# Earlier score copy, and latents modulated tile by tile beside the last context values

## The chip, the cores and the metric

The kernel runs on one core of a Trainium2 chip. The metric is the time of one execution on the device in microseconds (us). The engines, by the names of the profile, are PE (TensorE: matmuls), DVE (VectorE), ACT (ScalarE), POOL (GpSimd) and SP (SyncE, which here only issues transfers). Each engine runs its own instructions strictly in the order in which they were written. They meet through semaphores: an instruction waits until a counter has reached a value, and all behind it on that engine waits too.

## The reference, cut to what matters

Two blocks are computed on 256 tokens of width 2048. The first is a mixture of gating, dilated and sparse attention, cross attention and an MLP. Its output `x` goes into the second, and this is where the change lies:

```python
sh_m, sc_m, gt_m, sh_f, sc_f, gt_f = _modulation(c)        # silu(c) @ w_ada + b_ada, six parts
h_lat = x * (1.0 + sc_m) + sh_m                             # 256 latents
h_ctx = ctx * (1.0 + csc_m) + csh_m                         # 256 context tokens
q, k, v, log decays, g, p, bg = split(h @ w_in)             # for both; of the context k, v, decays matter
o_c, s_fwd, s_bwd = gla_two_way(context, zero state)        # chunks of 64, both directions
o_l, _, _ = gla_two_way(latents, s_fwd, s_bwd)
...                                                         # pooling branch, gates, norm, SwiGLU FFN (sh_f, sc_f, gt_f)
```

`o = q_inter @ state + scores @ v` within each head: the state's part is first formed as a small matrix of scores, and that matrix is then multiplied with the values.

## The kernel before, in words

**Weights.** All large products take weights that are streamed from memory in chunks of 1 MB (`RW`, five slots) and processed in halves of 512 KB. ACT rounds a half to a high part (`RH`, line 1194), DVE subtracts to get the low part (`RL`, line 2036), and PE multiplies both with the activations `A`, which are a pair of high and low too. One half is the clock of the whole program. `prepare` makes the parts four halves ahead of PE: the high part of half n+4 waits until PE has used half n-1, since there are five buffers. `gemm` is a product with columns of output on the partitions (lines 513 and 518, eight matmuls each). `gemm_n` is used for the values V, has tokens on the partitions and takes the tiles of `A` as stationary operand, two tiles (a pair) per half (lines 554, 556, 561).

**Order.** `schedule` is executed once for each engine and writes its instructions. `run` steps several generators in turn, and each `yield` ends a step, which as a rule holds one half of weights. What an engine writes in step n stands on it beside what the others write in step n. `beside=` is one more lane, stepped first. On ACT the products come ahead of the side work of a step (`weights_first`), on PE and DVE behind it. `slow(lane, 1.42)` steps a lane in two of three steps or so.

**The stretch in question.** After the context's modulation come `k2`, `low_rank`, and then a run of 45 steps: the products V, V, K, V, V of the context, beside four `ctx_head`s of 11 steps each (decays, sums, the state keys of a head, on ACT and DVE). Then the latents are modulated into `A` (`modulate(1, ...)`): for each of eight pairs of tiles DVE scales and shifts (line 2558, two instructions), ACT rounds to the high part (line 1659), DVE subtracts the low part (line 2548). `MODULATED` spreads this over six steps. `q2` then multiplies `A` with the first query weights; its first eight halves are zipped, block 0 and block 1 in turn, so that it needs pairs 0 and 1 for its halves 0 and 1, pairs 2 and 3 for halves 2 and 3, and so on (`need`). ACT waits before the first rounding until the last V product has used all of `A`.

Blocks alternate between two pairs of PSUM banks. A block waits (`block_begins`) until the block two before it is evacuated. After V products ACT does this (line 1690, two copies of 128x512); after `q2` and `k2` DVE does (line 2095) with a copy by ACT (line 1201) ahead of it.

**Fourth modulation sums.** `ada((4,), ...)` sums `silu(c) * w_ada` for one of the six parts: 32 transfers of 512 KB, each followed by one DVE instruction on 128x1024 (lines 2479, 2482). The number in `pauses` is how many steps lie between two of them. SP issues the transfer for item n+2 after item n is done (two slots), in its one queue, between the weight transfers. The result is needed only in the FFN; the lane is emptied before the latent heads.

**Latent heads.** `lat_head(h)` has two directions d; in each PE makes the scores inside chunks and then (line 1045) the scores of the state, in bank 5. ACT copies these from PSUM to `ST` (line 1828), and in the next step PE multiplies them with the state's values (line 1058). Before, the copy stands in the step after line 1045, behind that step's rounding of weights.

Of the kernel before, what the change touches and what calls it, by code (L numbers as in the profile page):

```python
# [129 lines left out]
class Banks:  # L130
# [11 lines left out]
    def next(self, signals=True):  # L142
        i = self.turn[self.at % len(self.turn)]
        self.at += 1
        return self.take(i, signals)
# [72 lines left out]
def chain(*lanes):  # L218
    for lane in lanes:
        yield from lane  # L220
# [8 lines left out]
def idle(n=0):  # L229
    for _ in range(n):  # L230
        yield
# [247 lines left out]
def tensor_program(nc, m, io):  # L479
# [3 lines left out]
    L = Lanes()  # L483
# [502 lines left out]
    def ctx_head(h):  # L986
        decay(0, h)
        decay(1, h)
        yield from idle(11)

# [190 lines left out]
def scalar_program(nc, m, io):  # L1181
# [470 lines left out]

    def modulate(use, tms):
        a.wait_ge(s["used"], num.last_of_a)
        for step in MODULATED:
            for p, low in step:
                if not low:
                    a.wait_ge(s["dm"], 8 * use + p + 1)
                    a.activation(m.A.high(2 * p, 2), pair2(tms[p % 2]), ACT.Copy).then_inc(s["dh"], 1)
            yield  # L1660

    def modulate_ctx():
        yield from modulate(0, m.x3_bufs[2:4])

# [18 lines left out]
    def v2():  # L1683
        n, dst = num.v, m.V[num.v % 2]
        num.v += 1

        def evac(b, g):
# [59 lines left out]
    def ctx_head(h):  # L1747
# [16 lines left out]
        yield  # L1764
        yield
        a.wait_ge(s["ks"], 2 * h + 2)
# [3 lines left out]
    def modulate_lat():  # L1770
        num.last_of_a = num.half
        yield from modulate(1, m.ON)

# [20 lines left out]
    def lat_head(h):  # L1794
# [5 lines left out]
        for d in range(2):  # L1800
# [21 lines left out]
            banks.next()  # L1822
            yield
            yield
        if num.on is not None:
            a.wait_ge(num.on.full, num.on.filled)
        a.wait_ge(s["qs"], 2 * h + 2)
        a.activation(m.ST, st.ap[:, :], ACT.Copy).then_inc(st.empty, 1)
        yield
# [195 lines left out]
def vector_program(nc, m, io):  # L2025
# [620 lines left out]
    def ctx_head(h):  # L2646
# [30 lines left out]
        yield  # L2677
        yield

# [410 lines left out]
def sync_program(nc, m, io):  # L3090
# [140 lines left out]
    L.v2 = lambda: gemm_n(1)  # L3231
    L.ctx_head = lambda h: idle(11)
    L.modulate_lat = L.alpha_x = lambda: idle(6)
# [35 lines left out]
def schedule(L):  # L3269
# [24 lines left out]
    L.low_rank(0)  # L3294
    beside = L.ada((4,), (2.25,))
    heads = chain(idle(1), L.ctx_head(0), L.ctx_head(1), L.ctx_head(2), L.ctx_head(3))
    run(*L.beside(heads, chain(L.v2(), L.v2(), L.k2(0, 2, 2), L.v2(), L.v2())), beside=beside)
    modulated = L.modulate_lat()
    next(modulated)
    run(*L.beside(modulated, L.q2()), beside=beside)  # L3300
    L.low_rank(1)
# [173 lines left out]
```

## Time and profile before

| | us |
|---|---|
| Three runs: median (lowest to highest) | 3023.03 (3022.83 to 3024.53) |
| Profiled execution: its own time | 3025.02 |
| Profiled execution: span of its instructions | 3023.7 |
| PE busy | 2941.7 (97%) |
| DVE busy | 2170.4 (72%) |
| ACT busy | 1454.5 (48%) |
| Mean granted clock of PE, as a share of full speed | 0.989 |

Busy time of PE counts overlapping matmuls once. Its 82 us of idle time lie in a few tens of waits, and the chain that ended last runs through PE for 91% of the span, so a microsecond that PE waits is a microsecond of the kernel's time, unless a later wait absorbs it. Idle time of the other engines costs nothing by itself. A row of a stretch has its bounds, its length, busy time (and number of instructions) of PE, of PE's weight loads, of DVE, ACT and POOL, then PE's granted clock as a share of full speed, the busy share of the DMA engines, and GB/s. A timeline row has the start, the duration from the first instruction's start to the last one's end, and in brackets the idle time before it with what ended it.

### The profile page before, as it was taken

How to read it: one execution, taken by the hardware profiler on the slowest of the kernel's cores; microseconds unless marked ns; L12 is line 12 of the kernel's file. 1: busy time of each engine (PE TensorE's matmuls, PEld its weight loads, DVE VectorE, ACT ScalarE, POOL GpSimd, SP SyncE). 2: the span in 40 equal slices, each digit the busy share in tenths (PEclk: the TensorE clock that was granted, in tenths of full speed). 3: DMA queues.
4: the chain of work that ended last, by engine and by line, in shares of the span. 5: the costliest groups of instructions: out<-in, count | busy, mean ns of one | idle time of the engine just before them, and what ended most of it. 6: DMA issues, size and time to landing. Idle time of an engine off the chain costs nothing.

```text
span 3023.7 us, 40090 instructions
## 1 busy us (share of the span) xinstructions
PE 2941.7 (97%) x16526; PEld 2545.6 (84%) x16526; DVE 2170.4 (72%) x2677; ACT 1454.5 (48%) x1941; POOL 8.5 (0%) x21
## 2 busy tenths in 40 slices
PE   8999999999999999998999999999999999999998
PEld 7888788888888888887887778888878888888886
DVE  5556767889899886789756656558888775555557
ACT  5445555544444444555444444544545444444444
POOL 0000000000000000000000000000000000000000
PEclk9999999999999999999999999999999999999999
DMA  6545234677677785577655445559646765555553
GB/s 251 194 168 195 98 140 151 233 263 260 257 264 265 288 316 208 183 273 273 257 185 181 167 163 190 192 216 344 226 160 251 280 249 183 193 183 193 185 191 112
DMA packets 107237, 648.61 MB, mean 215 GB/s; under 512 B 11920, under 2 KB 11920, under 8 KB 43440
## 3 DMA queue, kind: packets, MB, share of 16 engines
q1 hardware_dynamic: 99936, 621.86, 56.7%
q10 hardware_dynamic: 5184, 16.78, 1.4%
q0 software_dynamic: 1936, 7.41, 0.6%
q8 instruction: 131, 2.15, 0.3%
q14 instruction: 50, 0.41, 0.0%
HBM read 635.52 MB, written 10.49 MB: 214 GB/s over the span
## 4 chain that ended last, share of the span: by engine, by line
PE 91%; DVE 5%; ACT 2%; issue 1%; DMA 1%; SPq 0%; DVEq 0%; ACTq 0%
PE PS L513 50%; PE PS L518 26%; PE PS L554 3%; PE PS L556 3%; PE PS L561 3%; DVE RL L2036 1%; PE PS L791 1%; ACT RH L1194 1%; PE PS L1058 1%; PE PS L930 0%; PE PS L1045 0%; DMA RW<-in_w_ckv 0%; PE PS L976 0%; PE PS L582 0%; PE PS L693 0%
## 5 line engine op out<-in xcount | busy, mean ns | idle before, releaser
L2036 DVE TENSOR_TENSOR RL<-RW,RH 128x1024 fp32r<-128x1024 f32 x974 | 1177.9, 1222 | 544.7 <-ACT RH L1194 538.7
L1194 ACT ACTIVATE RH<-RW 128x1024 fp32r<-128x1024 f32 x974 | 1015.5, 1055 | 768.6 <-PE PS L518 652.0
L513 PE MATMUL PS<-A,RH 128*128 128x512 f32 x4544 | 1162.8, 398 | 35.0 <-ACT RH L1194 10.3
L513 PEld LDWEIGHTS PS<-A,RH 128*128 128x128 f32 x4544 | 827.1, 191 | 193.9 <-issue 37.8
L518 PEld LDWEIGHTS PS<-A,RL 128*128 128x128 f32 x4544 | 624.9, 192 | 45.4
L518 PE MATMUL PS<-A,RL 128*128 128x256 f32 x4544 | 637.9, 284 | 0.0
L513 PE MATMUL PS<-H,RH 128*128 128x512 f32 x2304 | 582.1, 395 | 1.2 <-ACT RH L1194 1.2
L513 PEld LDWEIGHTS PS<-H,RH 128*128 128x128 f32 x2304 | 416.2, 189 | 76.7 <-issue 1.4
L518 PEld LDWEIGHTS PS<-H,RL 128*128 128x128 f32 x2304 | 314.5, 190 | 22.7
L518 PE MATMUL PS<-H,RL 128*128 128x256 f32 x2304 | 321.3, 282 | 0.0
L1201 ACT ACTIVATE LT<-PS 128x512 f32<-128x512 f32 x232 | 138.2, 596 | 326.4 <-PE PS L518 326.3
L2482 DVE SCALAR_TENSOR_TENSOR G<-G,SILT 128x1024 f32<-128x1024 f32 x210 | 263.5, 1278 | 11.8 <-DMA G<-in_w_ada 11.7
L554 PE MATMUL PS<-RH,A 128*128 128x512 f32 x416 | 163.0, 392 | 0.0
L556 PE MATMUL PS<-RH,A 128*128 128x512 f32 x416 | 162.1, 390 | 0.0
L2095 DVE TENSOR_TENSOR G<-PS,LT 128x512 f32<-128x512 f32 x116 | 79.7, 687 | 72.8 <-ACT LT L1201 65.8
L561 PE MATMUL PS<-RL,A 128*128 128x512 f32 x416 | 111.2, 389 | 0.0
L554 PEld LDWEIGHTS PS<-RH,A 128*128 128x128 f32 x416 | 78.1, 188 | 17.8 <-issue 2.0
L561 PEld LDWEIGHTS PS<-RL,A 128*128 128x128 f32 x416 | 78.1, 188 | 16.3
L556 PEld LDWEIGHTS PS<-RH,A 128*128 128x128 f32 x416 | 78.1, 188 | 15.8
L1628 ACT ACTIVATE G<-G 128x512 f32<-128x512 f32 x32 | 20.2, 632 | 131.5 <-DVE G L2515 131.5
L1442 ACT ACTIVATE G<-G,SM 128x256 f32<-128x256 f32 (+1 forms) x56 | 24.8, 443 | 51.6 <-DVE SM L2287 51.6
L2404 DVE TENSOR_TENSOR X<-X,LT 128x512 f32<-128x512 f32 x56 | 38.5, 687 | 15.2 <-ACT LT L1201 15.2
(253 smaller groups left out, 1511.6 us busy)
## 6 DMA issues: line engine op xcount, KB each, us to landing
RW<-in_w_fin SPq DMA_DIRECT2D x88, 1024.0 KB, 4.8
G<-in_w_ada SPq DMA_DIRECT2D x160, 512.0 KB, 5.9
RW<-in_w_up SPq DMA_DIRECT2D x64, 1024.0 KB, 4.9
RW<-in_w_down SPq DMA_DIRECT2D x64, 1024.0 KB, 5.2
RW<-in_w_fout SPq DMA_DIRECT2D x44, 1024.0 KB, 4.7
RW<-in_w_v SPq DMA_DIRECT2D x32, 1024.0 KB, 4.9
RW<-in_w_bg SPq DMA_DIRECT2D x32, 1024.0 KB, 4.8
RW<-in_w_k SPq DMA_DIRECT2D x16, 1024.0 KB, 5.0
```

Source lines behind the costliest of these rows:

```text
L513: t.matmul(pair[mm][:, :], wh[:, k, mm * 128:mm * 128 + 128], x2(4 * c + k)[0], start=first and k == 0, stop=False, skip_group_check=True)
L518: done = t.matmul(pair[mm][:, 0:256], wl[:, k, mm * 128:mm * 128 + 128], x2(4 * c + k)[1], start=False, stop=last and k == 3, skip_group_c ...
L554: t.matmul(out[mm], hi(2 * c + k)[:, rows[mm]], wh[:, k, :], start=first and k == 0, stop=False, skip_group_check=True)
L556: t.matmul(out[mm], lo(2 * c + k)[:, rows[mm]], wh[:, k, :], start=False, stop=False, skip_group_check=True)
L561: done = t.matmul(out[mm], hi(2 * c + k)[:, rows[mm]], wl[:, k, :], start=False, stop=last and k == 1, skip_group_check=True)
L791: done = t.matmul(bk.ap[:, i * 128:i * 128 + 128], v, pt[0:n, j * 128:j * 128 + 128], start=x == 0, stop=x == len(ops) - 1)
L1194: a.activation(m.high(x), m.slot(j)[:, x % 2 * HC:x % 2 * HC + HC], ACT.Copy).then_inc(s["hi"], 1)
L1201: a.activation(pair2(m.LT[g % 2]), m.sum_l[g % 2], ACT.Copy).then_inc(s["lt"], 1)
L2036: v.tensor_tensor(m.low(x), m.slot(j)[:, x % 2 * HC:x % 2 * HC + HC], m.high(x).bitcast(F32), ALU.subtract).then_inc(s["lo"], 1)
L2095: v.tensor_tensor(pair2(out), m.sum_h[g % 2], pair2(m.LT[g % 2]), ALU.add).then_inc(m.pair[g % 2], 1)
L2404: stepped(v.tensor_tensor(x, x, m.LT[g % 2], ALU.add))
L2482: v.scalar_tensor_tensor(acc, m.ada_slot[cb][at], silu, acc, ALU.mult, ALU.add).then_inc(s["av"], 1)
```

## The change

Three things are done.

1. In `lat_head` ACT's copy of the score matrix moves up by one step, into the step in which PE makes the last of these scores (d == 1). The wait for `qs` stays with it.
2. `modulate_lat` no longer follows the context's V products but runs beside the last of them. `ctx_head` has 10 steps instead of 11 (an empty one is gone), so the fourth head ends after step 40, and the modulation takes steps 41 to 46; the last V has its halves in steps 36 to 43, and `q2` begins in step 45. Instead of one wait for the whole product, ACT waits for each pair p until the last V product has used its half p (`num.last_v + p + 1`), which is the half that reads pair p.
3. The pauses of the fourth modulation sums are 3.8 steps for the first ten of the 32, then 1.9, instead of 2.25 throughout.

```diff
     def ctx_head(h):
         decay(0, h)
         decay(1, h)
-        yield from idle(11)
+        yield from idle(10)
...
-    def modulate(use, tms):
-        a.wait_ge(s["used"], num.last_of_a)
+    def modulate(use, tms, free):
         for step in MODULATED:
             for p, low in step:
                 if not low:
+                    a.wait_ge(s["used"], free(p))
                     a.wait_ge(s["dm"], 8 * use + p + 1)
                     a.activation(m.A.high(2 * p, 2), pair2(tms[p % 2]), ACT.Copy).then_inc(s["dh"], 1)
             yield
 
     def modulate_ctx():
-        yield from modulate(0, m.x3_bufs[2:4])
+        yield from modulate(0, m.x3_bufs[2:4], lambda p: num.last_of_a)
...
     def v2():
         n, dst = num.v, m.V[num.v % 2]
         num.v += 1
+        num.last_v = num.half
...
         a.wait_ge(s["ks"], 2 * h + 2)
         a.dma_start(io["state"][h][:, 0:1024], m.KS).then_inc(l["spill"], 16)
...
     def modulate_lat():
-        num.last_of_a = num.half
-        yield from modulate(1, m.ON)
+        yield from modulate(1, m.ON, lambda p: num.last_v + p + 1)
...
             banks.next()
             yield
-            yield
-        if num.on is not None:
-            a.wait_ge(num.on.full, num.on.filled)
-        a.wait_ge(s["qs"], 2 * h + 2)
-        a.activation(m.ST, st.ap[:, :], ACT.Copy).then_inc(st.empty, 1)
+            if d == 1:
+                if num.on is not None:
+                    a.wait_ge(num.on.full, num.on.filled)
+                a.wait_ge(s["qs"], 2 * h + 2)
+                a.activation(m.ST, st.ap[:, :], ACT.Copy).then_inc(st.empty, 1)
+            yield
         yield
...
-    beside = L.ada((4,), (2.25,))
-    heads = chain(idle(1), L.ctx_head(0), L.ctx_head(1), L.ctx_head(2), L.ctx_head(3))
-    run(*L.beside(heads, chain(L.v2(), L.v2(), L.k2(0, 2, 2), L.v2(), L.v2())), beside=beside)
-    modulated = L.modulate_lat()
-    next(modulated)
-    run(*L.beside(modulated, L.q2()), beside=beside)
+    beside = L.ada((4,), (((10, 3.8), (22, 1.9)),))
+    heads = chain(idle(1), L.ctx_head(0), L.ctx_head(1), L.ctx_head(2), L.ctx_head(3), L.modulate_lat())
+    run(*L.beside(heads, chain(L.v2(), L.v2(), L.k2(0, 2, 2), L.v2(), L.v2(), L.q2())), beside=beside)
```

The order on DVE at the end of the fourth context head, before (L2644 and L2675 are the last work of the head, L2036 makes low parts, L2482 is a modulation sum, L2558 and L2548 modulate):

```order
L2644 TENSOR_TENSOR G<-G 128x512 x2
L2675 TENSOR_TENSOR G<-G,SM 128x512 x2
L2036 TENSOR_TENSOR RL<-RW,RH 128x1024
L2482 SCALAR_TENSOR_TENSOR G<-G,SILT 128x1024
L2036 TENSOR_TENSOR RL<-RW,RH 128x1024
L2482 SCALAR_TENSOR_TENSOR G<-G,SILT 128x1024
L2558 TENSOR_SCALAR G<-X,MODT 128x256 x4
L2548 TENSOR_TENSOR A<-G,A 128x2x256
L2558 TENSOR_SCALAR G<-X,MODT 128x256 x2
L2548 TENSOR_TENSOR A<-G,A 128x2x256
L2558 TENSOR_SCALAR G<-X,MODT 128x256 x2
L2548 TENSOR_TENSOR A<-G,A 128x2x256
```

And the same place in the changed program:

```order
L2644 TENSOR_TENSOR G<-G 128x512 x2
L2675 TENSOR_TENSOR G<-G,SM 128x512 x2
L2036 TENSOR_TENSOR RL<-RW,RH 128x1024 x2
L2558 TENSOR_SCALAR G<-X,MODT 128x256 x4
L2548 TENSOR_TENSOR A<-G,A 128x2x256
L2558 TENSOR_SCALAR G<-X,MODT 128x256 x2
L2548 TENSOR_TENSOR A<-G,A 128x2x256
L2036 TENSOR_TENSOR RL<-RW,RH 128x1024
L2482 SCALAR_TENSOR_TENSOR G<-G,SILT 128x1024
L2558 TENSOR_SCALAR G<-X,MODT 128x256 x2
L2548 TENSOR_TENSOR A<-G,A 128x2x256
L2036 TENSOR_TENSOR RL<-RW,RH 128x1024
```

Two modulation sums ahead of the modulation are gone, and between its steps there now stand low parts that belong to halves 1, 2, ... of `q2`.

The order on ACT around the evacuation of the last V product (L1690 before, L1691 after), first before:

```order
L1194 ACTIVATE RH<-RW 128x1024 [waits s_used]
L1690 ACTIVATE G<-PS 128x512 [waits s_used]
L1690 ACTIVATE G<-PS 128x512
L1696 DMA state<-G 128x1024 [waits l_spillv,s_pair1]
L1767 DMA state<-G 128x1024 [waits s_ks]
L1659 ACTIVATE A<-G 128x2x256 [waits s_dm,s_used]
L1659 ACTIVATE A<-G 128x2x256 [waits s_dm] x2
```

and after:

```order
L1767 DMA state<-G 128x1024 [waits s_ks]
L1194 ACTIVATE RH<-RW 128x1024 [waits s_used]
L1659 ACTIVATE A<-G 128x2x256 [waits s_dm,s_used] x3
L1194 ACTIVATE RH<-RW 128x1024 [waits s_used,l_w1]
L1659 ACTIVATE A<-G 128x2x256 [waits s_dm,s_used]
L1194 ACTIVATE RH<-RW 128x1024 [waits s_used]
L1659 ACTIVATE A<-G 128x2x256 [waits s_dm,s_used]
L1691 ACTIVATE G<-PS 128x512 [waits s_used]
L1691 ACTIVATE G<-PS 128x512
L1697 DMA state<-G 128x1024 [waits l_spillv,s_pair1]
```

The evacuation stood ahead of all of the modulation; now five of the eight roundings of tiles (pairs 0 to 4) stand in front of it.

The order on ACT in a latent head, as one piece each (L1201 copies low sums, L1828 before and L1827 after is the score copy, L1853 stores a gate):

```order
L1201 ACTIVATE LT<-PS 128x512 [waits s_used]
L1194 ACTIVATE RH<-RW 128x1024 [waits s_used,l_w1]
L1194 ACTIVATE RH<-RW 128x1024 [waits s_used]
L1853 DMA gate<-G 128x512 [waits s_pair1]
L1828 ACTIVATE G<-PS 128x512 [waits s_qs]
```

```order
L1201 ACTIVATE LT<-PS 128x512 [waits s_used]
L1194 ACTIVATE RH<-RW 128x1024 [waits s_used,l_w1]
L1827 ACTIVATE G<-PS 128x512 [waits s_qs]
L1194 ACTIVATE RH<-RW 128x1024 [waits s_used]
L1853 DMA gate<-G 128x512 [waits s_pair1]
```

The copy passes one rounding of weights and one transfer. The order on PE in the latent heads is unchanged.

## Rows read from the trace of the kernel before

**Rows 1.** Waits of PE: who waited for whom; us in total, times, longest us
```profile
PE PS L1058 <- ACT G L1828: 7.3, 4, 1.8
```

**Rows 2.** Timeline of PE, end of the last V product and start of `q2`
```profile
1410.72 1.07 PE L561 MATMUL PS<-RL,A 128*128 128x512 f32 x4
1413.44 1.07 PE L561 MATMUL PS<-RL,A 128*128 128x512 f32 x4
1424.11 3.75 PE L513 MATMUL PS<-A,RH 128*128 128x512 f32 x8 [9.60 <-DVE A L2548]
...
1429.37 2.27 PE L513 MATMUL PS<-A,RH 128*128 128x512 f32 x8
...
1432.42 2.00 PE L513 MATMUL PS<-A,RH 128*128 128x512 f32 x8
...
1435.22 2.00 PE L513 MATMUL PS<-A,RH 128*128 128x512 f32 x8
```

**Rows 3.** Busy and granted clock 1424.1 to 1428; timeline of PE, two other idle stretches
```profile
1424.10:1428.00 3.90, 3.89 (x10) 3.13 (x11) 3.79 (x8) 2.10 (x3) 0.00 (x0) 0.50 0.50 187
...
539.77 3.75 PE L513 MATMUL PS<-A,RH 128*128 128x512 f32 x8 [3.02 <-DVE A L2140]
...
2253.79 1.13 PE L1126 MATMUL PS<-X,C 128*128 128x256 f32 x4 [2.60 <-DVE X L2884]
```

**Rows 4.** Timeline of DVE, fourth context head and first steps of the modulation
```profile
1401.52 1.29 DVE L2482 SCALAR_TENSOR_TENSOR G<-G,SILT 128x1024 f32<-128x1024 f32 x1 [2.26 <-DMA G<-in_w_ada]
...
1417.12 1.22 DVE L2036 TENSOR_TENSOR RL<-RW,RH 128x1024 fp32r<-128x1024 f32 x1
1418.26 1.28 DVE L2482 SCALAR_TENSOR_TENSOR G<-G,SILT 128x1024 f32<-128x1024 f32 x1
...
1421.79 1.37 DVE L2558 TENSOR_SCALAR G<-X,MODT 128x256 f32<-128x256 f32 x4
...
1424.07 0.73 DVE L2558 TENSOR_SCALAR G<-X,MODT 128x256 f32<-128x256 f32 x2
...
1425.51 0.74 DVE L2558 TENSOR_SCALAR G<-X,MODT 128x256 f32<-128x256 f32 x2
```

**Rows 5.** Timeline of PE and ACT, end of the third V product, evacuation, roundings
```profile
1391.68 1.07 PE L561 MATMUL PS<-RL,A 128*128 128x512 f32 x4
...
1414.55 1.09 ACT L1690 ACTIVATE G<-PS 128x512 f32<-128x512 f32 x2 [1.65 <-PE PS L561]
...
1422.61 1.21 ACT L1659 ACTIVATE A<-G 128x512 fp32r<-128x512 f32 x2 [6.97 <-DVE G L2558]
```

**Rows 6.** Timeline around the score copy in the first and second latent head
```profile
1599.82 1.89 PE L1045 MATMUL PS<-G 128*128 128x256 f32 x8
...
1602.89 0.60 DVE L2767 TENSOR_TENSOR G<-G 64x128 f32<-64x128 f32 x2
...
1604.55 1.06 ACT L1194 ACTIVATE RH<-RW 128x1024 fp32r<-128x1024 f32 x1 [4.84 <-PE PS L518]
...
1605.51 0.58 ACT L1828 ACTIVATE G<-PS 128x512 f32<-128x512 f32 x1
...
1606.34 1.95 PE L1058 MATMUL PS<-G 128*128 128x512 f32 x4 [1.83 <-ACT G L1828]
...
1609.85 1.88 PE L1058 MATMUL PS<-G 128*128 128x512 f32 x4
...
1692.37 3.38 PE L1058 MATMUL PS<-G 128*128 128x512 f32 x4 [1.83 <-ACT G L1828]
...
1697.57 1.88 PE L1058 MATMUL PS<-G 128*128 128x512 f32 x4
```

**Rows 7.** DVE's groups from 1440 to 1560 us: count, busy, mean ns, idle before
```profile
L2036 DVE TENSOR_TENSOR RL<-RW,RH 128x1024 fp32r<-128x1024 f32 x42 | 51.0, 1223 | 29.5 <-ACT RH L1194 29.3
L2482 DVE SCALAR_TENSOR_TENSOR G<-G,SILT 128x1024 f32<-128x1024 f32 x11 | 14.1, 1282 | 7.0 <-DMA G<-in_w_ada 7.0
```

**Rows 8.** Waits of SP's queue from 1300 to 1480 us
```profile
SPq L3200 <- DVE G L2482: 15.1, 7, 4.7
```

More of the change, by code:

```diff
@@ L2677, in ctx_head @@
         yield
-        yield
     def modulate_lat():
@@ L3231, in sync_program @@
     L.v2 = lambda: gemm_n(1)
-    L.ctx_head = lambda h: idle(11)
+    L.ctx_head = lambda h: idle(10)
     L.modulate_lat = L.alpha_x = lambda: idle(6)
```

## The prediction

> **What bounds the kernel now.** I read the busy shares first: PE is busy for 97% of the span and holds 91% of the last chain, so the kernel gains only where PE stops waiting or runs faster. The waits of PE come next: the reader is to see that two of them are what this change touches, 9.6 us once (`q2` for the modulated tiles [rows 2]) and 7.3 us in four waits (the latent heads for the score copy [rows 1]). The timelines of these places then show what each costs beyond the waiting.
>
> At `q2`, PE ends the last V product at 1413.44 + 1.07 = 1414.51 and starts again at 1424.11 [rows 2]. The granted clock is 0.50 then [rows 3], the lower of its two levels (1.2 and 2.4 GHz): eight matmuls that take 2.00 us at 1435.22 take 3.75 [rows 2]. From 1424.11 to 1432.42 two halves take 8.31 us, while one half takes 1435.22 - 1432.42 = 2.80. So the slow clock costs 8.31 - 5.60 = 2.7 us, and the whole place 9.6 + 2.7 = 12.3 us.
>
> What ends last there is DVE, not the wait for `A`. ACT has been waiting for DVE's line 2558 for 6.97 us [rows 5], and DVE arrives at it only at 1421.79, seven microseconds after PE is done [rows 4], with the head's work, low parts and two modulation sums in between. DVE is behind since this stretch holds almost as much work for it as PE takes.
>
> **Part 1, the score copy.** In the first head PE ends line 1045 at 1599.82 + 1.89 = 1601.7, does half a chunk of weights, and is ready at 1606.34 - 1.83 = 1604.5. ACT has been idle for 4.84 us when that half ends, first rounds (1.06 us) and only then copies (0.58 us, until 1606.09) [rows 6]. The copy now stands ahead of the rounding, waits only for line 1045, and ends at about 1601.7 + 0.6 = 1602.3, that is 2.2 us before PE wants it. What is late next is DVE's line 2767, which ends at 1602.89 + 0.60 = 1603.5, still a microsecond early. So each of the four waits of 1.83 us goes whole: 7.3 us. The rounding behind the copy isn't late: it can't start before PE has used the half, at 1604.5, when ACT is free again. It costs nothing elsewhere, and the gate's transfer, which passes behind it, is not waited for in this step. In the second head the same wait was followed by slow matmuls: from line 1058 to its next group take 1697.57 - 1692.37 = 5.20 us against 1609.85 - 1606.34 = 3.51 in the first. With no idle stretch there I take these 1.7 us as regained. Part 1: 9.0 us; its bounds are 0 (another wait in the same place) and 9.0.
>
> **Part 2, the modulation.** Will it be ready? I lay DVE's new order end to end. In the changed order the third V product's decays on PE come three halves earlier, so the last half but one of that product ends one half pitch (1413.44 - 1410.72 = 2.72 [rows 2]) before its end at 1391.68 + 1.07 = 1392.75 [rows 5], at 1390.0. ACT's rounding (1.06) and DVE's low part (1.22) follow: DVE is free for the fourth head's sums at 1392.3, provided it has caught up, which fewer modulation sums in the first 35 steps should allow (30/3.8 = 8 sums against 30/2.25 = 13). From there:
> - Modulation sum to the end of the head's work: before 1417.12 - 1401.52 = 15.60 [rows 4], with four low parts; the new list has three, and one is 1418.26 - 1417.12 = 1.14. That leaves 14.46.
> - Two low parts 2.28, then the first step of the modulation (pairs 0, 1 and half of 2) 1425.51 - 1421.79 = 3.72. It ends at 1392.3 + 20.5 = 1412.8.
>
> PE wants pairs 0 and 1 at 1414.5. So the first half of `q2` starts without a wait, and the 9.6 us are gone. For pair 3, low part, sum 1.28, pair 1425.51 - 1424.07 = 1.44 and low part put it at 1417.8 to 1419, and PE wants it for half 2, at 1420.1. That holds too.
>
> A new wait stands beside it. Half 1 of `q2` is the first of block 1, and block 1 writes the PSUM banks of the last V product. Before, ACT evacuated them at once, at 1414.55 [rows 5]. Now that evacuation is queued behind ACT's rounding of pair 4, and that waits for DVE: 1412.8 + low part 1.14 + sum 1.28 + pair 1.44 + low part 1.14 + scale and shift 0.73 = 1418.5. Rounding 1.21/2 = 0.6, evacuation 1.09, and 0.25 until PE moves (1605.51 + 0.58 to 1606.34 [rows 6]) give 1420.4. PE is due at 1414.5 + 2.8 = 1417.3: it waits 3.1 us. It can hardly be less than 2.6, as DVE can't begin the list before 1392.3 and the list has no idle time in it; with one wait for data as the 2.26 us of rows 4 it is 5.4. I take 3.1.
>
> Does PE's clock fall in it? A stretch of 3.02 us at 539.77 was followed by eight matmuls in 3.75 us, the slow level; one of 2.60 us at 2253.79 by matmuls at full speed (1.13 for four) [rows 3]. The waits of 1.83 us in the first and second head fall on both sides [rows 6]. 3.1 us is nearest to the first, so I put 2.7 us more. The Trainium skill ("TensorE: Matmul & The Clock Gate", Part 1, What's actually happening) says that the gate's watch runs free of the kernel, so that where its transitions fall differs from run to run. The two equal waits of rows 6, only one with slow matmuls behind it, agree. By it the sum would be either with these 2.7 us or without them, which is the first rival below.
>
> Part 2: 12.3 - 3.1 - 2.7 = 6.5 us, bounds 4.2 (a wait of 5.4, slow) and 9.7 (2.6, full speed); with no wait at all 12.3.
>
> **Part 3, the sums.** Nothing is added: 32 transfers and 32 instructions as before. In the heads they are what lets DVE catch up (used above). After step 42 there is one each 1.9 steps. Per step DVE has a low part 1.22, 1.28/1.9 = 0.67 of sums and about 0.2 of evacuation, 2.1 us of 2.8 [rows 7]; in that stretch before, it was idle for 29.5 us waiting for roundings. I cost it at nothing, hidden by this. The last sum comes some eight steps later than before, still before the heads begin. Part of the bounds is rival 2.
>
> **Sum.** 9.0 + 6.5 = 15.5 us. Against the profiled execution's own 3025.0 us this is 3009.5; the median of the runs lies 2.0 us lower, at 3023.0, and gives 3007.5.
>
> **Rivals.**
> 1. *`q2` keeps its clock.* Same as the forecast, but the wait before half 1 is 2.6 to 3.1 us without slow matmuls behind it, or shorter since DVE is further ahead. For it: the 2.60 us stretch of rows 3. Gain 9.0 + 12.3 - 3.1 = 18.2 to 21.3 (no wait): 3001.7 to 3004.8.
> 2. *The dense sums make PE wait.* Each waits for its transfer as the worst does, 2.26 us [rows 4]: (1.28 + 2.26)/1.9 + 1.22 + 0.2 = 3.3 us per step against 2.8, 0.5 too much in some 38 steps, 19 us; four halves of reserve take 11.2 of them, and PE waits 7 to 8. Against it: the mean wait is 7.0/11 = 0.6 us [rows 7], with which a step has room. The transfers also delay each other: SP held its queue for 15.1 us in seven waits for DVE [rows 8], and weights stand behind these. The Trainium skill ("DMA: Bandwidth & Descriptors", Anatomy of one DMA) has a wait before a transfer held by the issuing sequencer, which speaks against denser sums in one queue with the weights; the row agrees. It would be this rival. Gain about 8: 3015.
> 3. *The score copy gains nothing,* since PE waits for another part of the same step (DVE's 2767, or the bank). Against it: the microsecond in hand above. Gain 6.5: 3016.5.
> 4. *Slower: `q2` stutters.* The modulation's steps have a low part, a pair and in every other step a sum on DVE, 1.14 + 1.44 + 1.28 = 3.9 us against 2.8. If DVE comes to step 41 more than four halves late (its reserve), PE waits before each of the first eight halves for low parts or pairs, about a microsecond each, and the clock stays at its lower level: eight halves at twice 2.8 are 22 us more, with the waits 30, less the 12.3 + 9.0 saved: 9 us slower, 3032. It decides from a start of the list at about 1397 instead of 1392.3. Against it: the load of the heads falls by six sums, and PE never waited there before.
>
> **Chances.** Forecast 0.50, rival 1 0.20, rival 2 0.15, rival 3 0.09, rival 4 0.04; 0.02 for nothing gained. Differences within 0.2% (6 us) can't be told from none here. Faster by more is the forecast, rivals 1 and 2, and half of rival 3 (it lies at the bound): 0.88. Within: 0.08. Slower: 0.04. The range 3002.5 to 3014.5 leaves out the best end of rival 1 and the worst of rivals 2 to 4.
>
> **What would show it.** Right: no wait of PE at line 1058; at `q2` no wait for line 2548, but one of about 3 us for ACT's evacuation of V (line 1691) ahead of the second half, with matmuls of 3.75 us per eight behind it; ACT's evacuation at about 1419 instead of 1414.6; DVE never idle from the fourth head's sums on. Wrong: a wait of PE for 2548 or for low parts inside `q2`; waits of PE from `q2` to the next V product, behind DVE's waits for transfers; a wait at 1058 with another releaser. My numbers fail first if DVE has not caught up at the fourth head, by as much as it is late.

## The result, and the profile after

| | median us (lowest to highest, runs) | ratio to before, 95% |
|---|---|---|
| before, same rounds | 3022.93 (3021.19 to 3026.64, 6) | |
| changed | 3014.19 (3010.64 to 3016.59, 6) | 0.9968 [0.9957, 0.9979] |
| changed, timed again with the last experiments | 3010.72 (3009.43 to 3011.66, 5) | 0.9963 [0.9950, 0.9975] |

The kernel is 8.7 us faster, in the second set 11.0. The forecast was 3007.5, so less came than was summed up. The profiled execution (3016.42 us, span 3015.1) shows where. First the waits of PE in it; the columns are those of [rows 1], waits of other places are left out:

```profile
PE PS L976 <- DVE ALR L2584: 4.5, 1, 4.5
...
PE PS L513 <- ACT G L1691: 2.8, 1, 2.8
PE PS L930 <- DVE G L2482: 2.7, 1, 2.7
```

The wait of [rows 1] at line 1058 is gone, and so is that of 9.60 us for line 2548 [rows 2]. The wait for 1691 is the one that was forecast. The other two are new in size or place: at line 976 PE had waited 1.1 us before, at line 930 not at all.

Now PE at the start of `q2`, which answers to [rows 2]:

```profile
1411.81 1.07 PE L561 MATMUL PS<-RL,A 128*128 128x512 f32 x4
1412.72 1.98 PE L513 MATMUL PS<-A,RH 128*128 128x512 f32 x8
...
1418.42 3.44 PE L513 MATMUL PS<-A,RH 128*128 128x512 f32 x8 [2.78 <-ACT G L1691]
...
1422.66 2.00 PE L513 MATMUL PS<-A,RH 128*128 128x512 f32 x8
```

The first half follows the V product without a gap. The second waits, and takes 1422.66 - 1418.42 = 4.24 us where the later ones take 2.79: 1.45 us of slow clock, not 2.7. ACT and, for the modulation, DVE in the same stretch answer to [rows 4, 5]:

```profile
1416.77 0.63 ACT L1659 ACTIVATE A<-G 128x512 fp32r<-128x512 f32 x1 [0.51 <-DVE G L2558]
1417.30 1.06 ACT L1691 ACTIVATE G<-PS 128x512 f32<-128x512 f32 x2
```

```profile
1407.69 1.38 DVE L2558 TENSOR_SCALAR G<-X,MODT 128x256 f32<-128x256 f32 x4
```

DVE starts to modulate 5.2 us before the V product ends at 1412.88. The evacuation, done at 1418.4, is queued behind the rounding of pair 4, as forecast.

The two places that weren't forecast: DVE's sums ahead of the low rank's copy (line 2584), PE behind it, and SP's transfers.

```profile
1451.59 1.28 DVE L2482 SCALAR_TENSOR_TENSOR G<-G,SILT 128x1024 f32<-128x1024 f32 x1 [1.27 <-DMA G<-in_w_ada]
...
1457.29 1.28 DVE L2482 SCALAR_TENSOR_TENSOR G<-G,SILT 128x1024 f32<-128x1024 f32 x1 [1.38 <-DMA G<-in_w_ada]
1458.49 1.22 DVE L2036 TENSOR_TENSOR RL<-RW,RH 128x1024 fp32r<-128x1024 f32 x1
1464.42 1.29 DVE L2482 SCALAR_TENSOR_TENSOR G<-G,SILT 128x1024 f32<-128x1024 f32 x1 [4.71 <-DMA G<-in_w_ada]
...
1471.41 0.42 DVE L2584 TENSOR_TENSOR ALR<-PS,ALR 128x256 f32<-128x256 f32 x1
```

```profile
1471.98 1.50 PE L976 MATMUL PS<-ALR,G 32*128 32x256 f32 x4 [4.47 <-DVE ALR L2584]
1473.41 3.78 PE L513 MATMUL PS<-A,RH 128*128 128x512 f32 x8
...
1523.74 1.94 PE L930 MATMUL PS<-C,G 128*128 128x128 f32 x8 [2.68 <-DVE G L2482]
```

```profile
1450.78 0.33 SPq L3105 DMA_DIRECT2D RW<-in_w_k  x1
1451.16 0.43 SPq L3199 DMA_DIRECT2D G<-in_w_ada  x1
1456.37 0.33 SPq L3105 DMA_DIRECT2D RW<-in_w_k  x1
1456.74 2.19 SPq L3199 DMA_DIRECT2D G<-in_w_ada  x2
1461.96 0.33 SPq L3105 DMA_DIRECT2D RW<-in_w_k  x1
```

In this stretch SP gets to a sum's transfer once per transfer of weights, every 5.59 us (1456.37 - 1450.78, 1461.96 - 1456.37), since it waits there for a slot of weights. With two slots, the transfer for the sum at 1464.42 could go as soon as the sum two before it was done, at 1451.59 + 1.28 = 1452.87; it goes at 1456.74, 3.9 us later. DVE wants it at 1464.42 - 4.71 = 1459.71 and it comes at 1464.4, 7.7 us after its issue, where the median is 6.0. What DVE has between the two sums is a single low part of 1.22 us. The groups of DVE from 1440 to 1560 us say the same in sum (counts and columns as in [rows 7]):

```profile
L2036 DVE TENSOR_TENSOR RL<-RW,RH 128x1024 fp32r<-128x1024 f32 x38 | 46.3, 1223 | 23.5 <-ACT RH L1194 23.2
L2482 DVE SCALAR_TENSOR_TENSOR G<-G,SILT 128x1024 f32<-128x1024 f32 x16 | 20.5, 1284 | 16.0 <-DMA G<-in_w_ada 15.8
```

Sixteen sums instead of eleven, and a mean wait of 1.0 us instead of 0.6. The two long waits among them are 4.71 and 4.02 us, each right ahead of a wait of PE; the others are 1.4 us or less. Finally the slow clock, by PE's granted clock in the stretches behind the three waits (columns as in [rows 3]):

```profile
1418.40:1421.70 3.30, 3.28 (x8) 2.65 (x9) 3.19 (x8) 1.35 (x2) 0.00 (x0) 0.55 0.72 235
1473.40:1478.70 5.30, 5.30 (x18) 4.52 (x17) 2.35 (x3) 2.73 (x4) 0.00 (x0) 0.50 0.13 51
1523.70:1527.70 4.00, 3.96 (x15) 3.53 (x16) 3.93 (x6) 0.00 (x0) 0.00 (x0) 0.57 0.44 170
```

At the score copy all is as forecast (answers to [rows 6]):

```profile
1603.00 0.60 ACT L1827 ACTIVATE G<-PS 128x512 f32<-128x512 f32 x1 [2.04 <-PE PS L1045]
1605.80 1.06 ACT L1194 ACTIVATE RH<-RW 128x1024 fp32r<-128x1024 f32 x1 [2.20 <-PE PS L518]
```

PE starts line 1058 at 1605.60, when it is ready, 2.0 us after the copy's end.

**The account by stretches.** PE's own marks cut the kernel in pieces in which all kernels do the same work: the groups at line 976 (low rank, context and latents) and the groups at line 1045. The starts of first and last come from the view of that line, here before and then changed:

```profile
L1045 PE MATMUL PS<-G x64: 377/379/382, 1572.6 to 1849.2; 128*128 128x256 f32 x64
```

```profile
L1045 PE MATMUL PS<-G x64: 377/379/382, 1573.9 to 1842.6; 128*128 128x256 f32 x64
```

Stretch A goes from the first L976 (context) to that of the latents, B from there to the first L1045, C from there to the last.

| kernel | median us | ratio, 95% | A | B | C | PE waits at q2 | 976 | 930 |
|---|---|---|---|---|---|---|---|---|
| before | | | 175.7 | 94.3 | 276.6 | 9.6 | 1.1 | 0 |
| changed | 3014.19 | 0.9968 [0.9957, 0.9979] | 171.0 | 101.9 | 268.7 | 2.8 | 4.5 | 2.7 |
| e11, the same | 3010.72 | 0.9963 [0.9950, 0.9975] | 169.9 | 101.7 | 268.7 | 2.8 | 3.2 | 2.7 |
| e1_copy_only | 3011.56 | 0.9961 [0.9947, 0.9974] | 173.6 | 95.9 | 268.7 | 8.6 | 1.1 | 0 |
| e2_sums_only | 3021.42 | 0.9990 [0.9981, 0.9999] | 173.0 | 95.9 | 276.6 | 6.6 | 1.1 | 0 |
| e4_evac_first | 3009.64 | 0.9954 [0.9942, 0.9967] | 167.4 | 98.8 | 268.7 | 1.6 | 3.4 | 2.7 |
| e5_pause_two | 3008.79 | 0.9950 [0.9938, 0.9963] | 173.4 | 95.9 | 268.7 | 7.2 | 1.1 | 0 |
| e6_even_sums | 3008.29 | 0.9949 [0.9937, 0.9962] | 169.5 | 94.3 | 268.7 | 4.6 | 1.1 | 0 |
| e7_gap_moved | 3008.23 | 0.9950 [0.9937, 0.9962] | 168.2 | 96.8 | 268.7 | 2.8 | 1.6 | 2.3 |
| e8_gap_and_evac | 3002.83 | 0.9940 [0.9926, 0.9953] | 163.6 | 96.9 | 268.7 | 0 | 1.1 | 2.4 |
| e9_fewer_sums | 3011.89 | 0.9967 [0.9954, 0.9979] | 167.7 | 104.1 | 268.7 | 0 | 5.5 | 4.2 |
| e10_even_evac | 3002.81 | 0.9938 [0.9924, 0.9951] | 164.4 | 94.3 | 268.7 | 0.7 | 1.1 | 0 |
| e12_quarter | 3007.61 | 0.9955 [0.9942, 0.9967] | 168.3 | 95.6 | 268.7 | 2.8 | 1.7 | 1.1 |
| e13_close_pair | 3010.33 | 0.9956 [0.9943, 0.9970] | 169.4 | 97.8 | 268.7 | 0.8 | 5.6 | 0 |

Ratios are to the kernel before in the same rounds. Its medians there were 3023.29 (e1 to e5), 3023.05 (e6 to e9), 3021.69 (e10 to e12) and 3021.93 (e13). The intervals of most changed kernels overlap with each other, so the medians alone hardly rank them. The stretches are of one profiled execution each and are the finer tool, since what lies ahead of A moves by up to 6 us with no change in the code (the first L976 starts at 1302.6 before, at 1296.2 in e8).

Changed against before, the spans differ by 8.6: 1.6 ahead of A, 4.7 in A, -7.6 in B, 7.9 in C, 2.0 behind it, where the fourth of the score waits lies.

### The profile page after: what moved, and what is told of

It reads as the page before. It is cut to its first block, busy times and chain, and to the rows that moved or that the text cites. A ratio compares the mean times of both kernels' runs of the same rounds, so it can differ in the third digit from the quotient of the medians.

```text
span 3015.1 us, 40101 instructions
## 1 busy us (share of the span) xinstructions
PE 2941.1 (98%) x16526; PEld 2546.4 (84%) x16526; DVE 2170.6 (72%) x2677; ACT 1454.7 (48%) x1941; POOL 8.5 (0%) x21
## 4 chain that ended last, share of the span: by engine, by line
PE 91%; DVE 5%; ACT 2%; DMA 1%; issue 1%; SPq 0%; ACTq 0%; DVEq 0%
PE PS L513 50%; PE PS L518 26%; PE PS L554 3%; PE PS L556 3%; PE PS L561 3%; DVE RL L2036 2%; PE PS L791 1%; ACT RH L1194 1%; PE PS L930 0%; DMA G<-in_w_ada 0%; PE PS L1045 0%; PE PS L1058 0%; PE PS L976 0%; DMA RW<-in_w_ckv 0%; PE PS L693 0%
## 5 line engine op out<-in xcount | busy, mean ns | idle before, releaser
L2036 DVE TENSOR_TENSOR RL<-RW,RH 128x1024 fp32r<-128x1024 f32 x974 | 1178.2, 1222 | 532.7 <-ACT RH L1194 526.6
L1201 ACT ACTIVATE LT<-PS 128x512 f32<-128x512 f32 x232 | 138.1, 595 | 326.6 <-PE PS L518 326.5
L2482 DVE SCALAR_TENSOR_TENSOR G<-G,SILT 128x1024 f32<-128x1024 f32 x210 | 263.6, 1279 | 16.9 <-DMA G<-in_w_ada 16.7
L556 PE MATMUL PS<-RH,A 128*128 128x512 f32 x416 | 162.5, 391 | 0.0
```

The source lines that it names most:

```text
L556: t.matmul(out[mm], lo(2 * c + k)[:, rows[mm]], wh[:, k, :], start=False, stop=False, skip_group_check=True)
L1201: a.activation(pair2(m.LT[g % 2]), m.sum_l[g % 2], ACT.Copy).then_inc(s["lt"], 1)
L2036: v.tensor_tensor(m.low(x), m.slot(j)[:, x % 2 * HC:x % 2 * HC + HC], m.high(x).bitcast(F32), ALU.subtract).then_inc(s["lo"], 1)
L2482: v.scalar_tensor_tensor(acc, m.ada_slot[cb][at], silu, acc, ALU.mult, ALU.add).then_inc(s["av"], 1)
```

## The experiments

**e1_copy_only.** The kernel before with the edit of `lat_head` alone.

> The kernel before with the score copy alone moved up (part 1). Theory: its four waits at line 1058 (7.3 us in four) go whole, and with them the slow matmuls behind the second of them (1.7 us), and nothing else changes: 9.0 us less than before, about 3014 us, all other waits of PE as before. Rival: the copy's gain in the changed kernel was 9 us only by chance of the clock, and what is regained is the waiting alone: 7.3 us. Second rival: most of the 8.7 us that the whole change gained came from here; then the other two parts together are worth about nothing, and this kernel is as fast as the whole change.

The second rival holds. C falls by 7.9 us and the fourth wait is gone too: part 1 is worth 9.7. This profile's span is 13.5 us shorter than before; of the rest, 3.0 us lie ahead of A, where the code is the same, and 0.5 us in A + B. Alone it is as fast as the whole change: the intervals of 0.9961 and of 0.9968 or 0.9963 overlap. So parts 2 and 3 together brought nothing that can be told, and in A + B the changed kernel is 2.2 to 3.4 us longer: 270.0 before, 269.5 here, 272.9 and 271.7 in the two profiles of the changed kernel.

**e2_sums_only.** The kernel before with the new pauses alone.

```diff
-    beside = L.ada((4,), (2.25,))
+    beside = L.ada((4,), (((10, 3.8), (22, 1.9)),))
```

> The kernel before with the new pauses of the fourth modulation sums alone (part 3). In the changed kernel PE waited 4.5 us at line 976 and 2.7 us at line 930. Theory A (a one-step gap): a wait of DVE over 4 us for a sum's transfer comes only where two sums stand one step apart, which the pause 1.9 does once in ten sums; here such gaps lie elsewhere than next to the low rank's copy, so line 976 waits about 1 us as before; one gap lies near the last sums, where PE may wait up to 3 us for line 930 or for low parts. Fewer sums in the heads let DVE reach the latents' modulation 3 to 5 us earlier, so the wait at q2 falls from 9.6 to 5 or 6 us. Sum: between 4 us faster and 1 us slower than before, 3019 to 3024. Theory B (the dense pace as such): DVE lags behind throughout the stretch after q2, PE waits at line 976 for over 3 us here too, and the kernel is 2 to 6 us slower than before.

Theory A as far as it goes: 6.6 us at q2, 1.1 at line 976, none at line 930, 0.9990 of the time. DVE's longest wait for a sum's transfer between 1440 and 1530 us is 3.1 us (at 1452.0, well ahead of the low rank), and PE doesn't notice it. The dense pace as such costs nothing here; B is 1.6 us longer by slow matmuls behind line 976 alone. The sums stand by a step or so otherwise to the rest than in the changed kernel; that this is why the long waits are missing is argued, not shown, by this run.

**e4_evac_first.** ACT's step table of `modulate`, latents only.

```diff
-        for step in MODULATED:
+        late = MODULATED[:2] + ((), MODULATED[2] + MODULATED[3]) + MODULATED[4:]
+        for step in late if use else MODULATED:
```

> The changed kernel, with ACT's rounding of latent pair 4 one step later, so that the evacuation of the last V product no longer stands behind it. Theory: PE's wait of 2.8 us for line 1691 ahead of q2's second half goes, and the slow matmuls behind it (4.24 us for a half that takes 2.79 elsewhere): 4.2 us faster than the changed kernel, 3010. ACT evacuates at about 1413 to 1414 us instead of 1417.3. Rival: PE then waits in the same place for what DVE or ACT finish next (low part or rounding of pairs 2 to 4, since the order of these is now tighter), and at most 1 us is gained. Second rival: only the waiting goes (2.8) and the clock's loss comes in another place.

Half right. Without the wait at L976, A is 167.4 - 3.4 = 164.0 against 171.0 - 4.5 = 166.5: 2.5 us instead of 4.2. PE still waits 1.6 us at q2, now without slow matmuls behind it (2.11 us for eight). ACT now waits at pair 3, which also stands ahead of the evacuation:

```profile
1415.44 0.63 ACT L1660 ACTIVATE A<-G 128x512 fp32r<-128x512 f32 x1 [2.28 <-DVE G L2559]
...
1416.93 1.06 ACT L1692 ACTIVATE G<-PS 128x512 f32<-128x512 f32 x2
```

**e5_pause_two.** The changed kernel with other pauses.

```diff
-    beside = L.ada((4,), (((10, 3.8), (22, 1.9)),))
+    beside = L.ada((4,), (((8, 3.8), (24, 2.0)),))
```

> The changed kernel with pauses of 3.8 steps for the first eight sums and of exactly 2 for the other 24, instead of 3.8 for ten and 1.9 for 22: as many sums, an almost equal pace, but no two of them one step apart. Theory A: the waits of DVE for a sum's transfer of 4.7 and 4.0 us go (none over 2.5 us is left), with them PE's waits at line 976 (4.5, back to about 1) and line 930 (2.7, to 0) and the slow matmuls behind both; 3.4 + 2.7 + 4 us = about 10 us faster than the changed kernel, 3004. Theory B (SP's one queue is full at this pace): the landing of each transfer stays at 5 to 6 us and DVE's waits only spread; PE waits in sum as long as in the changed kernel, 3012 to 3016.

Lines 976 and 930 are as theory A says: with no two sums one step apart, 3.4 us of wait go in A and 6.0 us in B. But 15 sums now stand up to step 47 instead of 13, DVE starts to modulate at 1413.01, when PE is done with V (1413.3), and q2 waits 2.2 + 4.9 us. Without the waits at line 976 A is 5.8 us longer than in the changed kernel (172.4 against 166.5), so that of 9.4 us 3.6 are left in A + B (269.3 against 272.9), not the 10 that were expected.

**e6_even_sums.** Parts 1 and 2, the old pause of 2.25.

> The changed kernel with the sums' old pause of 2.25 throughout: parts 1 and 2 without part 3. It has no two sums one step apart (2 or 3 steps always). Theory: parts 1 and 2 only work with the thin sums in the heads; with the old pause DVE begins the latents' modulation 4 to 6 us later than in the changed kernel (1407.7), so PE waits at q2 for line 2548 and for line 1691 for together 7 to 9 us, but not at line 930 and at line 976 only 1.1. Between the two L976 groups PE needs 173 to 176 us (before 175.7, changed kernel 171.0), from there to the first line 1045 about 96 (changed kernel 101.9). Time about that of the score copy alone, 3009 to 3013. Rival: the old pause is as good at q2 (the waits for transfers are rarer), q2 waits 3 us, and the kernel runs at 3004 to 3006.

A miss, and the most telling run. PE waits 4.6 us at q2, not 7 to 9, and never for line 2548. A + B is 263.8: part 2 is worth 5.7 to 6.3 us with the old pauses (against 269.5 in e1 and 270.0 before), and **part 3 costs 9.1 us** in the profiles (272.9 - 263.8; 7.9 by e11). The medians say the same less sharply, 5.9 us (2.4 against e11), and the intervals of the ratios overlap. DVE begins the modulation 3.4 us ahead of the end of V here (1405.90, end at 1409.26), against 5.2 with thin sums:

```profile
1404.70 1.28 DVE L2482 SCALAR_TENSOR_TENSOR G<-G,SILT 128x1024 f32<-128x1024 f32 x1
1405.90 1.38 DVE L2558 TENSOR_SCALAR G<-X,MODT 128x256 f32<-128x256 f32 x4
```

The thin sums were worth 1.8 us there. Without the waits at line 976 A is 1.9 us shorter with them (166.5 against 168.4).

**e7_gap_moved.** As many sums up to the modulation, then `(9, 2.0), (1, 1.0), (2, 2.0), (1, 1.0), (8, 2.0)` (pairs of count and pause).

> The changed kernel with as many sums before and beside the modulation as it has, and the later ones two steps apart, but for two one-step gaps that are put two and seven steps behind the low rank's products instead of right ahead of them and at the last sums. Theory A: a sum's transfer that comes late hurts only where PE needs DVE at once (the low rank's copy, line 2584, and the last sum, line 2482, ahead of line 930); elsewhere the four halves of reserve take it. DVE still waits 4 us or so at the moved gaps, but PE doesn't: line 976 about 1.1, line 930 none; q2 as in the changed kernel (2.8 us for line 1691, no wait for 2548). From L976 to L976 167 to 168 us, from there to the first line 1045 96: about 9 us faster than the changed kernel, 3005. Theory B: late transfers cost PE the same wherever they stand; new waits of PE for low parts (line 2036) or line 2095 of 3 us each appear, and nothing is gained.

Line 976 falls to 1.6 us, near what theory A has, and there are no new waits for low parts. The 4 us waits of DVE at the moved gaps, which the theory expected, don't come: DVE has one or two low parts between these sums, and waits 0.6 us at most. So this run doesn't test whether PE would have taken a late transfer there; e9 does. Line 930 still waits 2.3 us, though the last sums stand two steps apart: near the end of the V product these steps hold no low part on DVE. DVE and SP there:

```profile
1517.01 0.68 DVE L2095 TENSOR_TENSOR G<-PS,LT 128x512 f32<-128x512 f32 x1
1521.41 1.29 DVE L2482 SCALAR_TENSOR_TENSOR G<-G,SILT 128x1024 f32<-128x1024 f32 x1 [3.73 <-issue]
```

```profile
1515.35 0.43 SPq L3199 DMA_DIRECT2D G<-in_w_ada  x1
```

DVE is ready for the last sum at 1517.7, 2.3 us after its transfer's issue, and gets it 6.1 us after the issue. So the distance that counts is DVE's time between two sums, not the number of steps. A + B is 7.9 us shorter than in the changed kernel, 265.0 against 272.9.

**e8_gap_and_evac.** As e7, with the sums' pauses of e7, and ACT's rounding of pair 3 behind the evacuation as well.

```diff
+        late = MODULATED[:1] + ((), (), MODULATED[1] + MODULATED[2] + MODULATED[3]) + MODULATED[4:]
```

> As e7_gap_moved, and ACT's roundings of latent pairs 3, 4 and 5 stand behind the evacuation of the last V product (in e4_evac_first only pair 4 and 5 did, and ACT still waited 2.28 us for DVE's pair 3 ahead of it). Theory: ACT evacuates at about 1414, as soon as PE is done, PE has no wait at q2 for line 1692 and keeps its clock, and pairs 3 to 5 are rounded in time, since PE wants them only from its third half on. From L976 to L976 163 to 164 us. 4 us faster than e7_gap_moved, 3001. Rival: the low parts of pair 3 or those of the weights, which DVE can make only after ACT's later roundings, become the new wait (line 2549 or 2037), and it is as fast as e7_gap_moved or slower.

As expected: A without its wait at L976 falls from 166.6 to 162.5, about the 4.2 that the wait and the slow matmuls at q2 had cost (4.1). The median falls by 5.4 us. ACT evacuates at once, and PE has neither a wait nor a slow matmul there:

```profile
1408.44 1.06 ACT L1692 ACTIVATE G<-PS 128x512 f32<-128x512 f32 x2
```

```profile
1407.02 1.07 PE L561 MATMUL PS<-RL,A 128*128 128x512 f32 x4
1407.92 1.98 PE L513 MATMUL PS<-A,RH 128*128 128x512 f32 x8
...
1410.69 2.00 PE L513 MATMUL PS<-A,RH 128*128 128x512 f32 x8
```

**e9_fewer_sums.** As e8, no sum between steps 39 and 46 (the changed kernel has two there), the later ones shifted.

> As e8_gap_and_evac, with no sum for seven steps (39 to 46) around the start of the latents' modulation and one more one-step gap later. Theory: DVE has one sum (1.28 us) less ahead of pair 3, so what is left of waits at q2 is up to 1.3 us shorter; if e8_gap_and_evac has none left there, it is as fast as that, 3000 to 3001. Rival: the third gap costs PE a wait of its own, and it is slower.

Slower, as the rival has it, and more: the shift puts the sums ahead of the low rank and the last ones where DVE has only a short instruction between two of them, PE waits 5.5 and 4.2 us there, and 9 us are lost against e8. A long wait of DVE stands between these two places as well:

```profile
1498.51 1.28 DVE L2483 SCALAR_TENSOR_TENSOR G<-G,SILT 128x1024 f32<-128x1024 f32 x1 [4.49 <-issue]
```

PE doesn't stop from line 976 to line 930 (1523.60). This is the third one-step gap (steps 72 and 73), so the rival has the direction and not the cause. A wait of DVE of 4 to 5 us costs PE nothing here, and about its whole length where PE wants DVE's next result.

**e10_even_evac.** Parts 1 and 2, the old pause, and e8's order on ACT.

> Parts 1 and 2 with the sums' old pause of 2.25 (as e6_even_sums), and ACT's roundings of latent pairs 3, 4 and 5 behind the evacuation of the last V product (as e8_gap_and_evac). Theory: e6_even_sums lost 4.6 us at q2 to line 1691 and some 1.5 us of clock, and nothing at lines 976 and 930; e8_gap_and_evac lost nothing at q2 and 2.4 us at line 930. So both together lose nothing at either: from L976 to L976 163.5 us, from there to the first line 1045 94.3 to 95.9, in sum 258 to 259.5, against 270.0 before, 272.9 in the changed kernel, 260.4 in e8_gap_and_evac. Time about 3001, the fastest of all. Rival: DVE is 1.8 us later at the modulation with the even sums (its first step began 3.4 us ahead of the end of the V product instead of 5.2), and q2 now waits for low parts of pairs 2 or 3 (line 2549), about 1 to 2 us: 3003.

A + B is 258.7, the least of all. PE waits 0.7 us at q2, for ACT's evacuation and not for low parts, so the rival's mechanism isn't seen; its time, 3003, is nearer than the 3001 that was expected. The time is 3002.8, as for e8, 7.9 us below the changed kernel in the same rounds. Of the kernels tried this is the one to take: it also needs no new table of pauses.

**e11_change_again.** The changed kernel once more.

> The changed kernel as it is, timed in the same rounds as the others. All theories: 3014 us as before, and again waits of PE of 3 to 5.5 us at line 976, 2.8 us for line 1691 and 2 to 3 us at line 930.

The three waits come again (3.2, 2.8, 2.7 us); the time is 3.5 us lower than in the first set.

**e12_quarter.** Small transfers for the sums.

```diff
+                part = 256 if cb == 4 and n >= 2 else 1024
-                y.dma_start(slots[n % len(slots)], io["w_ada"][16 * cb + kt][:, 1024 * w:1024 * w + 1024]).then_inc(
-                    l[f"a{n % len(slots)}"], 16)
+                y.dma_start(slots[n % len(slots)][:, 0:part],
+                            io["w_ada"][16 * cb + kt][:, 1024 * w:1024 * w + part]).then_inc(l[f"a{n % len(slots)}"], 16)
```

> The changed kernel, in which the transfers of the fourth modulation sums from the third on bring a quarter of the columns (128 KB instead of 512 KB), so that three quarters of these weights are left out; the instructions, their order and the pauses are the same. Theory A (a sum's transfer is late because 1 MB of weights and two sums of 512 KB stand in the queues together): the transfers land 2 to 3 us after their issue, DVE's waits of 4.7 and 4.0 us fall under 1.5, PE waits about 1.1 us at line 976 and not at line 930; 8 to 9 us faster than the changed kernel, 3005. Theory B (they are late because SP issues them late, when DVE has freed the slot, and a transfer behind the weights takes its time whatever its size): DVE's wait ahead of the low rank stays over 3 us and PE's at line 976 with it; 3012 to 3014.

In between. The wait ahead of the low rank falls from 4.7 to 2.9 us, the last one from 4.0 to 2.9, and PE's to 1.7 and 1.1. The median is 3.1 us below e11 in the same rounds; in A + B it is 7.8 us (263.9 against 271.7), of which 4.9 are lost again ahead of A (1301.4 against 1296.5), where the first L976 starts. The issues in the stretch from 1420 to 1530 us, changed kernel and e12 (count, size of one, median us to landing):

```profile
G<-in_w_ada SPq DMA_DIRECT2D x18, 512.0 KB, 6.0
RW<-in_w_k SPq DMA_DIRECT2D x8, 1024.0 KB, 5.1
```

```profile
G<-in_w_ada SPq DMA_DIRECT2D x19, 128.0 KB, 4.7
```

A quarter of the size takes four fifths of the time. What stands ahead of the transfer counts more: one that SP issued 6.7 us behind the last megabyte landed after 4.0 us in the changed kernel (issued at 1419.63) and after 2.7 us in e12 (1420.08). So the size is worth 1.3 us, and coming right behind 1 MB 2.0 us, with either size; these two are single transfers. The time from the slot's being free to the issue (3.9 us above) comes on top. So both theories hold in part.

The Trainium skill ("DMA: Bandwidth & Descriptors", Anatomy of one DMA) has about 2.0 us fixed and 436 GB/s for a transfer, measured on GpSimd's path; an estimate from it is 3.2 us for 512 KB alone and 2.3 for 128 KB, and with the megabyte ahead served first 5.6 and 4.7 us. The rows agree roughly: 4.0 and 2.7 alone, 6.0 and 4.7 behind the megabyte.

**e13_close_pair.** e10 with the sums of steps 59 and 61 at 60 and 62.

> The kernel e10_even_evac with two of its 32 sums one step later, those at steps 59 and 61 now at 60 and 62; the next stands at 63 as before. On DVE the last sum ahead of the low rank's copy is then separated from the one before by a single short instruction (line 2096) instead of low parts of weights; the pace as a whole stays even and low. Theory (close pair): that sum waits 3 to 5 us for its transfer, which SP can issue only once per weight transfer, and since the low rank's copy follows in order, PE waits 3 to 5.5 us at line 976 instead of 1.1, with slow matmuls behind it; all else as in e10_even_evac (163.5 to 164.4 us from L976 to L976 become 167 to 169). 4 to 6 us slower than e10_even_evac, 3007. Rival (pace): what made PE wait in the changed kernel was the many sums in this stretch; with the old pace one close pair is absorbed by what DVE is ahead, PE waits 1 to 2 us at line 976 and the time stays 3003.

Theory, and harder than expected: two of 32 sums moved by one step cost 7.5 us in the median (3010.33 against 3002.81, each with its own rounds; no run of one is within the range of the other, though the intervals of the ratios touch) and 5.0 + 3.5 = 8.5 us in A + B. DVE, PE and SP of it:

```profile
1460.33 1.28 DVE L2483 SCALAR_TENSOR_TENSOR G<-G,SILT 128x1024 f32<-128x1024 f32 x1 [1.04 <-DMA G<-in_w_ada]
1461.53 0.68 DVE L2096 TENSOR_TENSOR G<-PS,LT 128x512 f32<-128x512 f32 x1
1466.41 1.28 DVE L2483 SCALAR_TENSOR_TENSOR G<-G,SILT 128x1024 f32<-128x1024 f32 x1 [4.19 <-issue]
```

```profile
1470.90 2.04 PE L976 MATMUL PS<-ALR,G 32*128 32x256 f32 x4 [5.59 <-DVE ALR L2585]
1472.88 3.78 PE L513 MATMUL PS<-A,RH 128*128 128x512 f32 x8
```

```profile
1454.55 0.43 SPq L3200 DMA_DIRECT2D G<-in_w_ada  x1
1459.76 0.33 SPq L3106 DMA_DIRECT2D RW<-in_w_k  x1
1460.13 1.84 SPq L3200 DMA_DIRECT2D G<-in_w_ada  x2
```

The releaser is given as "issue", but the sum starts 6.3 us after the first of the two issues at 1460.13, as late as the others land; that it waits for the transfer is read from this, not from the releaser.

## Why the prediction was right or wrong

**Right in sign and, just so, in range; right in mechanism for parts 1 and 2 and wrong for part 3.** The forecast time was too low by 6.7 us (3.2 in the second set). That the first median lies within the range is in part luck: its upper bound is 3014.5, 0.3 us away, and a gain of part 1 above its bound stands against a loss that the sum didn't have. The parts by the account, forecast against measured gain:

- *Part 1: 9.0, measured 7.9 + 1.8 to 2.0 = 9.7 to 9.9.* All four waits went, DVE's line 2766 ended 0.9 us ahead of PE (1604.13 + 0.60 against 1605.60; "a microsecond early"). The clock behind them gave 2.4 to 2.6 instead of 1.7, which put the gain above the stated bound of 9.0.
- *Part 2: 6.5, measured 6.3 alone* (e6 against before, A + B), *8.1 with the thin sums ahead of it* (A without the waits at L976: 174.7 to 166.5). In the changed kernel the wait was 2.8 us for 3.1, and the clock's term 1.45 for 2.7. That the V evacuation is what ends last is shown by e8, where the wait and the slow matmuls go together with it.
- *Part 3: 0, measured -9.1* against the old pauses. This is the step that failed: "I cost it at nothing, hidden by this". The share of busy time was right (the idle time in front of low parts is still 23.5 us), but a mean over the stretch doesn't say what happens at two points of it. There two sums stand close on DVE while their transfers are bound to SP's 5.59 us rhythm, and behind them PE wants DVE at once, with none of the four halves of reserve. The changed kernel pays 3.4 us (4.5 - 1.1) at line 976 and 2.7 at line 930, and 4.9 of slow clock behind them (B is 7.6 longer, of which 2.7 is the wait): 11.0 us, less the 1.9 that the thin sums gave in A. And "in the heads they are what lets DVE catch up" was worth these 1.9 us (e6), not the condition of the gain.

So in the profiles 9.8 + 6.3 - 9.1 = 7.0 us, and 1.6 ahead of A, where the code is the same, make the 8.6 of the spans. Of the signs that the prediction named for being wrong, one came: waits of PE between `q2` and the next V product, behind DVE's waits for transfers.

Of the rivals, the second is what happened: it named SP's queue and DVE's waits for the sums, its price was 7 to 8 us and its time 3015. But its mechanism, each sum waiting as the worst until the reserve is used up, is not what the trace shows. Most sums in the dense part wait 1.4 us or less and PE doesn't notice; e5 (no two sums one step apart, none of the two waits), e9 and e13 show that it is the place. The third rival fell with e1. The first (`q2` keeps its clock) failed: in all four profiles with this wait of 2.8 us (changed, e11, e7, e12) slow matmuls follow. The fourth fails too: no kernel with part 2 is slower than before.

What is partly open: the waits at line 976 differ between two profiles of the same kernel (4.5 and 3.2 us) by just as much as the time that the late sum's transfer took from its issue, 7.7 us (1464.42 - 1456.74) and 6.4 (1458.91 - 1452.50 in e11). Why one took longer isn't known. Whether a third slot for the sums, so that SP can issue earlier, would make the dense pace harmless wasn't tried.

## What to carry to other kernels

A side lane with its own transfers is hidden only if each of its instructions is, so before its pace is changed, look not at the mean slack but at the points where the main engine needs that engine's very next result, and count what stands between the lane's last two instructions ahead of them. A PSUM evacuation that frees a bank belongs ahead of work that waits for a third engine; moved there it was worth 4 us for one table entry. And when a change has several parts, time each alone: here the first paid for the whole gain, and the third cost more than the second saved.

## What the runs showed of the hardware

Whether the clock falls after a short wait isn't settled by the place and the length of the wait. Behind 1.07 us at line 976, in e1 and in e10:

```profile
1473.26 1.10 PE L976 MATMUL PS<-ALR,G 32*128 32x256 f32 x4 [1.07 <-DVE ALR L2585]
1474.29 3.43 PE L513 MATMUL PS<-A,RH 128*128 128x512 f32 x8
```

```profile
1465.04 1.10 PE L976 MATMUL PS<-ALR,G 32*128 32x256 f32 x4 [1.07 <-DVE ALR L2585]
1466.06 2.12 PE L513 MATMUL PS<-A,RH 128*128 128x512 f32 x8
```

B is 95.9 with the slow matmuls (e1, e2, e5) and 94.3 without (before, e6, e10). And behind the 3.02 us at 536 to 540 us, which I took for the sign that three microseconds bring the slow level [rows 3], the same eight matmuls take 2.06 us in e8. The code up to this point is the same in all kernels:

```profile
536.14 2.06 PE L513 MATMUL PS<-A,RH 128*128 128x512 f32 x8 [3.02 <-DVE A L2141]
```

Over the fourteen profiles they take 3.4 to 3.75 us in seven (before, changed, e2, e4, e5, e7, e12), 2.5 to 2.6 in two (e1, e10) and 2.06 to 2.08 in five (e6, e8, e9, e11, e13). At other places the profiles agree: the wait of 2.8 us at `q2` was followed by slow matmuls each time, in four. One profile is no evidence for whether a wait costs its clock; several of the same place are.
